# Triangular inverses of two mixers on 32x32 diagonal blocks, four tiles of the array in place of two 64x64 tiles

## The reference

```python
a_kk = jnp.einsum('bnhid,bnhjd->bnhij', kb, k) * jnp.exp(jnp.where(strict, seg, -jnp.inf))
rhs = jnp.concatenate([kb * jnp.exp(gcum)[..., None], v * beta[..., None]], axis=-1)
sol = lax.linalg.triangular_solve(a_kk, rhs, left_side=True, lower=True, unit_diagonal=True)
...
v_new = u_n - w_n @ s
o_n = q_n @ s + aqk_n @ v_new
s = s * gl_n[..., None, None] + jnp.swapaxes(k_n, -1, -2) @ v_new
```

```python
sz = jnp.einsum('bhvk,bhk->bhv', s, z_t)
s = (s * w_t[:, :, None, :] + sz[..., None] * b_t[:, :, None, :] + v_t[..., None] * k_t[:, :, None, :])
return s, jnp.einsum('bhvk,bhk->bhv', s, r_t)
```

## Time and profile before

| | before |
|---|---|
| median of 3 runs | 2915.53 us (2914.61 to 2920.76) |
| span of the profiled execution | 2922.9 us, the one time that its page has |
| TensorE busy | 2601.6 us, 89% |
| TensorE's weight loads | 1471.9 us |
| VectorE busy | 1537.2 us, 53% |
| ScalarE busy | 985.8 us, 34% |
| GpSimd busy | 835.3 us, 29% |

### The profile page before, as it was taken

One profiled execution on the slowest core, in us unless ns is written; L12 is line 12 of the kernel. 1 busy time (PEld: TensorE's weight loads), 2 busy tenths in 40 slices (PEclk: granted clock), 3 DMA queues, 4 the chain that ended last, 5 costly groups with the idle time before them and its releaser, 6 DMA issues. The chain is left out here.

```text
span 2922.9 us, 78835 instructions
## 1 busy us (share of the span) xinstructions
PE 2601.6 (89%) x30395; PEld 1471.9 (50%) x30396; DVE 1537.2 (53%) x2779; ACT 985.8 (34%) x1687; POOL 835.3 (29%) x654
## 2 busy tenths in 40 slices
PE   5999899799789779788888987989999999999956
PEld 2448358455788745588874434333333333333322
DVE  3106375654366522444443466666666666666628
ACT  2603116212222113222211111445555555555511
POOL 1000000000333100111100000556666666666655
PEclk9999998899999889999998999999999999999988
DMA  6001302300000020000013213889898989782277
GB/s 248 1 13 38 127 15 87 105 15 1 3 4 4 3 70 0 2 4 4 4 43 112 87 55 125 325 336 349 350 367 316 355 327 344 269 315 92 79 288 309
DMA packets 109125, 408.53 MB, mean 140 GB/s; under 512 B 21001, under 2 KB 37083, under 8 KB 83932
## 3 DMA queue, kind: packets, MB, share of 16 engines
q1 hardware_dynamic: 76636, 287.71, 26.6%
q0 software_dynamic: 20736, 75.51, 6.7%
q10 hardware_dynamic: 11520, 41.95, 3.6%
HBM read 346.40 MB, written 58.72 MB: 139 GB/s over the span
## 5 line engine op out<-in xcount | busy, mean ns | idle before, releaser
L3287 PE MATMUL bank<-arena 128*32 x1280 | 568.7, 597 | 9.6 <-SPq L68 6.7
L3289 PE MATMUL bank<-arena 128*32 128x512 f32 x3840 | 569.8, 597 | 0.0
L3248 POOL COPY arena<-arena 128x2048 f32 x240 | 448.8, 1904 | 329.3 <-PE bank L3321 312.3
L1348 PE MATMUL bank<-arena 64*64 64x64 f32 x8320 | 277.4, 219 | 69.7 <-DVE arena L1444 19.7
L3287 PEld LDWEIGHTS bank<-arena 128*32 128x32 f32 x1280 | 134.9, 110 | 358.5 <-issue 349.5
L1348 PEld LDWEIGHTS bank<-arena 64*64 64x64 f32 x8320 | 260.1, 135 | 81.5 <-DVE arena L1444 22.4
L3318 PE MATMUL bank<-arena 128*32 x640 | 289.2, 595 | 5.5 <-POOL arena L3248 5.5
L3321 PE MATMUL bank<-arena 128*32 128x512 f32 x1920 | 290.3, 595 | 0.0
L3442 DVE COPY arena<-arena 128x2048 f32 x80 | 138.4, 1731 | 200.5 <-PE bank L3289 183.6
L3379 ACT COPY arena<-arena 128x2048 f32 x80 | 152.0, 1900 | 200.1 <-PE bank L3289 143.5
L3238 POOL DMA_INDIRECT arena<-normed_rows,arena x80 | 166.1, 2076 | 149.6 <-DVE arena L3426 137.8
(11 more groups left out here) (561 smaller groups left out, 4550.0 us busy)
## 6 DMA issues: line engine op xcount, KB each, us to landing
arena<-in_exp_w_gate_dram SPq DMA_DIRECT2D x64, 1024.0 KB, 6.1
arena<-in_exp_w_up_dram SPq DMA_DIRECT2D x64, 1024.0 KB, 8.8
arena<-in_exp_w_down_dram SPq DMA_DIRECT2D x64, 1024.0 KB, 9.5
expert_rows<-arena ACTq DMA_DIRECT2D x80, 512.0 KB, 8.2
arena<-in_w_mod_dram SPq DMA_DIRECT2D x32, 512.0 KB, 7.7
arena<-in_x_dram SPq DMA_DIRECT2D x16, 512.0 KB, 6.6
arena<-in_w_mod_dram SPq DMA_DIRECT2D x8, 1024.0 KB, 18.4
arena<-in_w_in_dram SPq DMA_DIRECT2D x12, 384.0 KB, 5.3
```

Of the source, the lines that this page charges most:

```text
L1348: last = self.nc.tensor.matmul(self.banks[bank][r, x * HD:(x + 1) * HD], lhsT[r, x], rhs[r, x], start=True, stop=True)
L3248: last = nc.gpsimd.tensor_copy(down_copy(u), down_of(slots[u]))
L3287: nc.tensor.matmul(out(SUB - 1), XTT[:, b.q, c, rows(SUB - 1)], W[:, :, c], start=first, stop=end)
L3289: last = nc.tensor.matmul(out(u), XTT[:, b.q, c, rows(u)], WC[:, u, :, c], start=first, stop=end)
```

## The change

`Solve` computes stages 0 to 6 only on the 32x32 diagonal blocks. A system's two diagonal blocks lie on two strips of 32 partitions, so four strips hold two systems' blocks, packed: the work tiles `M`, `N`, `X`, `T` and the new `C` (which takes Y's place in these stages) are 8 x 32 columns instead of 8 x 64. A product is now 32 matmuls of 32x32 by 32x32, 8 column blocks on four strips, each on the diagonal tile of the array that belongs to its strip. Stage 7 multiplies the off-diagonal block of N64 from one strip to the other (quad g to quad g ^ 1), and stage 8 writes X times the unit and X times T next to each other, so that it is 64 matmuls; VectorE then copies the whole bank to Y once, 128x512, in place of the addition. All other evacuations are 128x256. `Halves` gets a packed unit matrix and four small copies a mixer for it. The class `Inverse`, which nothing calls, goes; line numbers after it fall by 74 or so. GpSimd's masks, the weaving and all else stay.

```diff
+QD = HD // 2
+
+def quad(g):
+    return slice(QD * g, QD * g + QD)
+
+def own(g):
+    return slice(QD * (g % 2), QD * (g % 2) + QD)
+
+def other(g):
+    return slice(QD * (1 - g % 2), QD * (1 - g % 2) + QD)
...
-            last = nc.vector.tensor_copy(self.ident[r], k.ident[r, r])
+            nc.vector.tensor_copy(self.ident[r], k.ident[r, r])
+            for g in (2 * a, 2 * a + 1):
+                last = nc.vector.tensor_copy(self.unit[quad(g)], k.ident[quad(g), quad(g)])
...
-        self.M, self.N, self.X, self.T = (cr.take(8, HD) for _ in range(4))
+        self.M, self.N, self.X, self.T, self.C = (cr.take(8, QD) for _ in range(5))
...
-    def product(self, bank, lhsT, rhs):
+    def blocks(self, bank, lhsT, rhs):
         for x in range(8):
-            for a in range(2):
-                r = half(a)
-                last = self.nc.tensor.matmul(self.banks[bank][r, x * HD:(x + 1) * HD], lhsT[r, x], rhs[r, x],
+            for g in range(4):
+                r = quad(g)
+                last = self.nc.tensor.matmul(self.banks[bank][r, x * QD:(x + 1) * QD], lhsT(r, g, x), rhs(r, g, x),
                                              start=True, stop=True)
...
-            self.product(0, self.M, self.N)
-            self.product(1, self.N, self.M)
-            last = self.product(2, self.N, Y)
+            self.blocks(0, M, N)
+            self.blocks(1, N, M)
+            last = self.blocks(2, N, C)
...
         elif k == 7:
             self.dve_done(pe, p, 6)
-            last = self.product(1, N64, Y)
+            for x in range(8):
+                for g in range(4):
+                    to = quad(g ^ 1)
+                    last = self.nc.tensor.matmul(self.banks[1][to, x * QD:(x + 1) * QD], N64[quad(g), x, other(g)],
+                                                 self.C[quad(g), x], start=True, stop=True)
         else:
             self.act_done(pe, p, 7)
-            last = self.product(2, self.X, self.T)
+            for x in range(8):
+                for col, rhs in ((own, unit), (other, T)):
+                    for g in range(4):
+                        r, at = quad(g), x * HD + col(g).start
+                        last = self.nc.tensor.matmul(self.banks[2][r, at:at + QD], self.X[r, x], rhs(r, g, x), start=True,
+                                                     stop=True)
...
-        b = [bank[:, :].rearrange("p (x j) -> p x j", x=8) for bank in self.banks]
+        b = [bank[:, 0:8 * QD].rearrange("p (x j) -> p x j", x=8) for bank in self.banks]
...
+        elif k == 8:
+            last = self.nc.vector.tensor_copy(self.Y[:, p % 2], self.banks[2].rearrange("p (x j) -> p x j", x=8))
         else:
-            if k >= 3:
-                self.dve_done(dve, p, {3: 2, 4: 3, 6: 4, 8: 6}[k])
-            else:
-                self.dve_done(dve, p, 0)
-            last = TT(Y, Y, b[2], ALU.add)
+            self.dve_done(dve, p, {2: 0, 3: 2, 4: 3, 6: 4}[k])
+            last = TT(C, C, b[2], ALU.add)
```

More of the change, by code:

```diff
@@ L1309, in __init__ @@
         self.b16, self.l32, self.l64, self.ident = (cr.take(HD) for _ in range(4))
+        self.unit = cr.take(QD)
     def build(self, nc, k, chain):
@@ L1342, in dve_done @@
         eng.wait_ge(self.dve_s, p * self.NDVE + self.DVE_AT[k] + 1)
-    def product(self, bank, lhsT, rhs):
+    def blocks(self, bank, lhsT, rhs):
         for x in range(8):
-            for a in range(2):
-                r = half(a)
-                last = self.nc.tensor.matmul(self.banks[bank][r, x * HD:(x + 1) * HD], lhsT[r, x], rhs[r, x],
[L1349 to L1354, removed]
-                r = half(a)
-                last = self.nc.tensor.matmul(self.banks[bank][r, x * HD:(x + 1) * HD], src[r, x], self.c.ident[r],
+            for g in range(4):
+                r = quad(g)
+                last = self.nc.tensor.matmul(self.banks[bank][r, x * QD:(x + 1) * QD], lhsT(r, g, x), rhs(r, g, x),
                                              start=True, stop=True)
@@ L1360, in tensor @@
     def tensor(self, pe, k, p):
-        N0, N32, N64, Y = (b[:, p % 2] for b in (self.N0, self.N32, self.N64, self.Y))
+        N0, N32, N64 = (b[:, p % 2] for b in (self.N0, self.N32, self.N64))
+        packed = lambda b: lambda r, g, x: b[r, x]
+        level = lambda b: lambda r, g, x: b[r, x, own(g)]
+        unit = lambda r, g, x: self.c.ident[r, own(g)]
+        M, N, X, T, C = (packed(b) for b in (self.M, self.N, self.X, self.T, self.C))
         if k == 0:
@@ L1364, in tensor @@
                 self.dve_done(pe, p - 1, 6)
-            last = self.turn(0, N0)
+            last = self.blocks(0, level(N0), unit)
         elif k == 1:
             self.act_done(pe, p, 0)
-            self.product(0, self.M, N0)
-            last = self.product(1, N0, self.M)
+            self.blocks(0, M, level(N0))
+            last = self.blocks(1, level(N0), M)
         elif k == 2:
@@ L1385, in tensor @@
             self.dve_done(pe, p, 3)
-            last = self.product(2, self.N, Y)
+            last = self.blocks(2, N, C)
         elif k == 5:
             self.dve_done(pe, p, 4)
-            self.turn(0, Y)
-            last = self.product(1, N32, Y)
+            self.blocks(0, C, unit)
+            last = self.blocks(1, level(N32), C)
         elif k == 6:
```

11 lines of the change are left out of this document (5 added, 6 removed).

## The result

The change made the kernel slower: 3154.24 us, median of 4 runs (3152.63 to 3158.02), beside 2918.15 us for the kernel before in the same session; ratio 1.081, 95% interval 1.080 to 1.083. The prediction was 2831 us, with a range from 2798 to 2922. It was wrong by 323 us and in sign.

The account below looks back on a forecast made before the run. It took TensorE, with VectorE's and ScalarE's chains in three places, as the bound. Savings of 3.2 us a delta rule pair and 5.2 an RWKV pair, ten pairs each, made 84 us: 2915.5 to 2831 us, range 2798 to 2922.

Parts of the forecast that it names:

- What bounds the kernel: Delta rule and RWKV loops: TensorE is busiest, 29 ns a record; in three places a faster TensorE makes nothing start earlier.
- three places: Delta rule stages 3 and 7 wait for VectorE's chains; RWKV stage 2 for a chain through ScalarE and VectorE.
- Part 1: Interval between records of 32x32 matmuls in the inverse: 32 ns a tile, 8.0 ns with four at once, 0.51 us a product.
- its formula: Within a tile, the interval follows its columns, loaded ones too: 52 ns less for 64 fewer.
- Rival 3: In the loops, waits fall elsewhere or instructions, needed at twice the rate, come late: 24 us less gain, 2855 us; chance 0.12.
- Rival 2's end: In the inverse's products, a fixed 29 ns a record, 1.86 us a product, some 3200 us; chance 0.03 for 25 or 29 ns.
- a floor of 25 ns: Between any two TensorE records, at least 25 ns: 3049 us; chance 0.03 for 25 or 29 ns.
- Part 2: Between the inverse's 32x32 blocks and 64x64 work, a tile switch costs TensorE 0.09 us each way, bounds 0 and 0.2.
- Part 3: The inverse's evacuations, all but the last, shrink to 128x256: 0.69 to 0.42 us on VectorE, 0.60 to 0.37 on ScalarE.
- the walk: Stretch by stretch through a late pair: delta rule 25.7 to 22.5 us, RWKV 31.6 to 26.4.
- What would show it wrong: In the loops: blocks short but pairs not, or a granted clock below the 0.94 and 0.99 of before.

Follow-up runs that it names:

- the merged kernel: Changed kernel with stage 2's N times M and C in one matmul, and stage 8's X times unit and T in one: 3059.86 us, ratio 1.048.
- the bench: Kernel before with thirteen appended stretches of TensorE matmuls, written out or looped; 512 of 32x32 took 3.66 us per 256 instructions written out, 14.75 us in all as a loop.
- the split kernel: Kernel before with each 64x64 matmul of `product` given as two of 32 moving columns: 3260.8 us, ratio 1.121.
- the second bench: Kernel before with fourteen other appended TensorE stretches, varying moving columns, tile switches and loop lengths; 64x32 and 64x64 compared, a switch took 0.14 us.

## Why the prediction was wrong

Step by step:

- **What bounds the kernel.** Right as far as it went: TensorE, and in three places VectorE's and ScalarE's chains. It left out the third bound. The demand could be read before: q8's 178 packets, and 1538 and 1858 records a pair in 25.75 and 31.83 us, 16.7 and 17.1 ns an instruction, 17% and 20% above the 14.3 of the supply. The limit itself, 14.3, stood in no row of before.
- **Part 1, s = 8.0 ns.** Nearly right at full clock, 8.7 ns over 116 records; at 0.50, some 14 ns, which the prediction had no term for. The reading of its formula that the experiments began with, loaded and moving columns added up, is wrong: 64 loaded and 32 moving take 29 ns a record on two tiles, as long as 64 and 64. The prediction's own row had it: L1548, with one moving column, takes 31 ns. In the merged kernel 32 loaded and 64 moving take 14 ns on four tiles (L1299, 62 records in 1.07 us, the last one's 0.22 in it), 56 ns a tile; so the wider of the two sets the interval. For 32 and 32 both give the same.
- **The failed step** is the one from s to the product and the pair, "with four tiles at once s = 8.0 ns and 0.51 us a product", and "16 products of 32 matmuls, 64 records each" counted only as array time. A product's 64 records are 128 instructions, half a packet: 1.83 us of supply, where the product of before, 64 instructions, needed 0.92, just its 0.93 on the array. In place of pairs of 22.5 and 26.4 us the runs showed 38.8 and 44.2, at 14.8 and 15.0 ns an instruction. The rows that I took for the small tile's interval were stretches of 32 records and of 3, both shorter than a packet, and none could show a rate of supply.
- **Rival 3** named it, "the instructions, needed at twice the rate, come late", and priced it at 24 us less gain without a row. By the count it is (2624 - 1536) x 14.3 ns = 15.6 us a pair of supply, less the slack of a pair (25.75 - 22.0 = 3.8; 31.8 - 26.5 = 5.3): 11.8 and 10.3 us more. Measured: 13.0 and 12.4. The rest, 1 to 2 us a pair, I put down to stretches that wait for a chain while the supply has no room to run ahead; that is argued, not shown. Another candidate is the lower clock: the 64x64 stretches between the blocks take 53 ns a record at 0.50, more than the supply's 28.6, so there the array is late and not the program. No run tells the two apart.
- **Rival 2's end**, a fixed 29 ns a record, gave "some 3200", at a chance of 0.03 that it shared with a floor of 25 ns, and the measured 3154 lies close to it. That is luck: the interval on the array was 8.7 ns, and it is the supply that makes 28.6 ns of a record and its load.
- **Part 2, the switch.** 0.14 us and not 0.09, inside the bounds, and of little weight beside 12 us a pair.
- **Part 3 and the chains.** Right in kind and close in size in the loops when tried alone (1.23 and 1.66 us a pair, 1.35 and 1.29 in the walk). In the changed kernel it can have given little, since few chains are late any more: of TensorE's 171.1 us of idle time ahead of L1270, 142.5 are "issue", and VectorE idles 200.2 us ahead of L1368. No run had the wide evacuations there.
- **What would show it wrong.** Both signs came: blocks short and pairs not, and a granted clock of 0.74 and 0.81. Of the second I had thought as a cause; the bench's two clocks show that the pace of the supply doesn't hang on it. It goes with TensorE's standing still: the same 32x32 matmuls had 0.50 written out and 0.89 in a loop. That standing still is the only thing that lowers it isn't so, as the split kernel and the second bench's 64x32 loop show.

In sum, 18 intervals between the ten pairs' starts hold 309.5 - 217.4 = 92 us (delta rule) and 385.6 - 280.3 = 105 us (RWKV; starts of gram_k and of gram_t) of the difference of the spans, 233 us; the rest lies in the last pairs and in the parts around the loops, which run the same inverse.

## What to carry to other kernels

Before a change that multiplies small matmuls, count the instructions, and not the columns: fp32 takes four a matmul, and written-out code comes at 256 instructions in 3.6 us here, so any stretch longer than a packet whose instructions take the array under 14.3 ns each is bound by its own program. Idle time with "issue" as its cause that recurs every 128 matmul records is the sign; the q8 row and records per microsecond are the check ahead of time. Fewer and wider matmuls lift it (77 to 94 us here), and so does a hardware loop of up to some 1600 instructions, which was tried in the bench alone and costs 0.2 to 0.3 us at each trip's branch; smaller tiles don't.

## What the runs showed of the hardware

- The supply of TensorE's program: 3.66 us a packet of 256 instructions at a granted clock of 0.50, 3.57 at 0.92. A loop of 1600 instructions is fetched once, one of 1700 in every trip.
- Within a tile the wider of loaded and moving columns sets the interval: on two 64x64 tiles 64x32 and 64x64 both take 29 ns a record at a clock of 1.00 and 53 ns at 0.50.
- In the second bench a loop of these 64x32 matmuls kept TensorE busy throughout and yet ran at a granted clock of 0.50, 1.2 GHz, while the same loop with 64 moving columns had 0.98. Why isn't shown. First the one, then the other:

```profile
2978.00:3141.00 163.00, 163.00 (x3062) 163.00 (x3061) 0.00 (x0) 0.00 (x0) 0.00 (x0) 0.50 0.00 0
...
3207.00:3298.00 91.00, 91.00 (x3071) 90.93 (x3068) 0.00 (x0) 0.00 (x0) 0.00 (x0) 0.98 0.00 0
```

- A switch between 32x32 and 64x64 tiles costs TensorE 0.14 us.
